# The u half of the spatial gate computed inside the attention, eight more merge gates in block products, and the two output projections run one after the other

## The reference

```python
h = rmsnorm(x, norm_mix_g)
q, kv, nsa_g, u, v, merge_g = split(h @ w_in)         # u, v: 1024 wide; merge_g: 2 x 2048
o_a = nsa_attention(q, compressed/selected/window k and v, sigmoid(nsa_g))      # 512 x 1024
v   = layernorm(gelu(v))                               # over 1024
o_b = gelu(u) * (tril(ws) @ v_chunk + bs)              # 8 groups of 128, chunks of 128 tokens
g   = sigmoid(merge_g)                                 # two branches
merged = g[0] * (o_a @ w_proj_a) + g[1] * (o_b @ w_proj_b)
x = x + merged @ w_mix_out
... cross attention over 256 memory tokens, SwiGLU, final norm
```

## Time and profile before

| | us |
|---|---|
| median of 3 runs | 2754.77 (2754.28 to 2754.85) |
| profiled execution | 2755.36 |
| its span | 2753.6 |
| TensorE busy in the span | 2712.6 (99%) |
| VectorE, ScalarE, GpSimd busy | 2105.9, 1209.4, 454.7 |

### The profile page before, as it was taken

How to read it: one execution, slowest core, us unless ns; L and a number is a source line. 1 busy time by engine, 2 the same in 40 slices (tenths; PEclk the granted TensorE clock), 3 DMA queues, 4 the chain that set the end, 5 groups by cost and what they waited for, 6 DMA issues and landing times.

```text
span 2753.6 us, 38090 instructions
## 1 busy us (share of the span) xinstructions
PE 2712.6 (99%) x14221; PEld 2301.0 (84%) x14221; DVE 2105.9 (76%) x2998; ACT 1209.4 (44%) x1923; POOL 454.7 (17%) x418
## 2 busy tenths in 40 slices
PE   8999999999999999999999999999999999999997
PEld 7888888888888888888877888888888888888886
DVE  6777874667755555555687899999999998988887
ACT  6444432766631222211154555555555555443334
POOL 0000002545520545411000000000000000010000
PEclk9999999999999999999999999999999999999999
DMA  7587867332233455444345788888889888999982
GB/s 240 139 187 177 205 157 171 81 89 62 54 96 104 102 145 150 133 115 114 92 142 138 172 216 198 218 208 212 196 214 215 207 207 250 300 305 297 302 262 93
DMA packets 647978, 479.38 MB, mean 174 GB/s; under 512 B 14484, under 2 KB 589320, under 8 KB 641928
## 3 DMA queue, kind: packets, MB, share of 16 engines
q1 hardware_dynamic: 568016, 416.58, 51.9%
q0 software_dynamic: 58896, 36.70, 10.2%
q10 hardware_dynamic: 20904, 23.92, 2.9%
HBM read 413.98 MB, written 63.18 MB: 173 GB/s over the span
## 4 chain that ended last, share of the span: by engine, by line
PE 85%; DVE 5%; ACT 3%; issue 2%; POOL 2%; DMA 2%; ACTq 0%; DVEq 0%; SPq 0%; POOLq 0%
PE banks L1405 10%; PE banks L1408 10%; PE banks L1406 9%; PE banks L976 9%; PE banks L978 9%; PE banks L977 9%; PE banks L1470 4%; PE banks L1472 4%; PE banks L1471 4%; PE banks L1074 3%; PE banks L1077 3%; PE banks L1075 3%; PE banks L1236 1%; PE banks L1237 1%; PE banks L1238 1%
## 5 line engine op out<-in xcount | busy, mean ns | idle before, releaser
L1487 DVE CAST w_hi<-raw 128x512 fp32r<-128x512 f32 (+1 forms) x232 | 141.5, 610 | 244.2 <-PE banks L978 171.4
L976 PE MATMUL banks<-act_hl,w_hi 128*128 128x512 f32 (+1 forms) x816 | 324.1, 397 | 2.5 <-DVE w_lo L1508 2.4
L977 PE MATMUL banks<-act_hl,w_hi 128*128 128x512 f32 (+1 forms) x816 | 319.0, 391 | 0.0
L978 PE MATMUL banks<-act_hl,w_lo 128*128 128x512 f32 (+1 forms) x816 | 318.9, 391 | 0.0
L1406 PEld LDWEIGHTS banks<-t_hl,wf_lo 128*128 128x128 f32 x1312 | 246.5, 188 | 58.1
L1405 PE MATMUL banks<-t_hl,wf_hi 128*128 128x512 f32 x656 | 259.5, 396 | 0.1
L1408 PE MATMUL banks<-t_hl,wf_hi 128*128 128x512 f32 x656 | 259.5, 396 | 0.0
L1406 PE MATMUL banks<-t_hl,wf_lo 128*128 128x256 f32 x1312 | 257.7, 278 | 0.0
L1940 DVE TENSOR_TENSOR wf_lo<-raw_f,wf_hi 128x1024 fp32r<-128x1024 f32 x164 | 200.3, 1221 | 55.8 <-ACT wf_hi L2586 55.7
L2586 ACT ACTIVATE wf_hi<-raw_f 128x1024 fp32r<-128x1024 f32 x164 | 173.8, 1060 | 137.6 <-PE banks L1408 82.0
L1406 PEld LDWEIGHTS banks<-tok_hl,wf_lo 128*128 128x128 f32 x984 | 184.9, 188 | 43.7
(11 more groups left out here) (357 smaller groups left out, 6574.1 us busy)
## 6 DMA issues: line engine op xcount, KB each, us to landing
raw_f<-in_w_ffn_in_dram SPq DMA_DIRECT2D x82, 1024.0 KB, 9.0
raw<-in_w_in_dram SPq DMA_DIRECT2D x42, 1024.0 KB, 5.6
h_full<-hidden_blocks SPq DMA_DIRECT2D x35, 1024.0 KB, 8.2
wo_raw<-in_w_ffn_out_dram SPq DMA_DIRECT2D x32, 1024.0 KB, 9.9
raw_g<-in_w_in_dram SPq DMA_DIRECT2D x26, 1024.0 KB, 8.7
hidden_blocks<-tok_hl SPq DMA_DIRECT2D x44, 512.0 KB, 6.3
s<-in_w_ffn_in_dram SPq DMA_DIRECT2D x40, 512.0 KB, 6.0
s<-in_w_ffn_in_dram POOLq DMA_DIRECT2D x40, 512.0 KB, 6.5
```

The source lines that it names most:

```text
L976: pe.matmul(dst, w_hi[:, q, j, 0:m], hi, start=first, stop=False)
L977: pe.matmul(dst, w_hi[:, q, j, 0:m], lo, start=False, stop=False)
L978: return pe.matmul(dst, w_lo[:, q, j, 0:m], hi, start=False, stop=last)
```

## The change

- The 8 panels of u move from `su` into the fill of the attention. Their raw result goes to DRAM (`su_dram`) and is loaded again by `rows_in`, as a fourth transfer of 256 KB behind the three small ones; GELU is then applied in place on SBUF.
- For them, 8 merge gates leave the fill and become 4 more pairs of block products (13 pairs become 17, 91 units become 119). The rotating buffers are renumbered.
- `su` is gone. `ab` is split in `pa` (all 16 half panels of branch a) and then `pb` (16 of branch b). The work of the 8 groups runs beside `pa`; PE mixes group n after half panel 2, 4, 5, 7, 9, 10, 12, 14.
- DVE multiplies each bank by its gate (`part_a`, `part_b`); POOL only adds and makes the low part. The gates come in 1 MB transfers of four tiles, and ACT applies the sigmoid tile by tile (`open_gate`): two tiles in each of the 8 rounds of the groups, four before the last group's copy, the rest beside `pb`.

```diff
-G_TILES = [...] + [("merge", n) for n in range(PLAIN_GATES, PLAIN_GATES + 10, 2)]
+G_TILES = [...] + [("merge", n) for n in range(PLAIN_GATES, PLAIN_GATES + 18, 2)]
+MIX_AT = {h: g for g, h in enumerate((2, 4, 5, 7, 9, 10, 12, 14))}
-        ("merge", (2 * DK - GATES_AHEAD,)), ("sv", (8,)), ("su", (8,)), ("ab", (16, 4, 2, 2)), ("wo", (16,)),
+        ("fill", (SG + 2 * DK - GATES_AHEAD,)), ("sv", (8,)), ("pa", (8, 4, 2, 2)), ("pb", (8, 4, 2, 2)), ("wo", (16,)),
...
 # SP
+            def gates_in(m):
+                b, c = divmod(m, 4)
+                if m >= 2:
+                    sp.wait_ge(gates_open, 4 * (m - 1))
+                if b:
+                    sp.wait_ge(banks_read, PH["pa"].group0 + 4 * c + 4)
+                rows = (b * DK + 4 * c) * P
+                sp.dma_start(gate_in[:, 4 * c:4 * c + 4], merge_dram[rows:rows + 4 * P].rearrange("(k p) t -> p k t", p=P)).then_inc(gates_landed[m % 2], 16)
...
 # PE
+            def half_panel(ph, h, hi, lo, ready, free=None):
+                pe.wait_ge(banks_read, ph.group0 + h - 1 if free is None else free)
...
+                for q in range(2):
+                    if h == 0:
+                        pe.wait_ge(ready, 4 * q + 4)
...
+            for h in range(16):
+                half_panel(PH["pa"], h, oa_hi, oa_lo, oa_lo_done, PH["sv"].group0 + TC if h == 0 else None)
+                if h in MIX_AT:
+                    mix(MIX_AT[h])
+            for h in range(16):
+                half_panel(PH["pb"], h, ob_hi, ob_lo, ob_lo_done)
...
 # DVE
+            def part_a(h):
+                dve.wait_ge(quarters_done, PH["pa"].quarter0 + 2 * h + 2)
+                dve.wait_ge(gates_open, h + 1)
+                dve.tensor_tensor(pa[:, h], bank[(PH["pa"].group0 + h) % 2][:], gate_in[:, h], ALU.mult).then_inc(banks_read, 1)
...
+            for h in range(16):
+                quarter_split(4 + 2 * h)
+                part_a(h)
+                quarter_split(5 + 2 * h)
+                if h == 14:
+                    dve.wait_ge(mix_copied, SG)
...
+            for h in range(16):
+                if h < 14:
+                    quarter_split(36 + 2 * h)
+                part_b(h)
+                if h < 14:
+                    quarter_split(37 + 2 * h)
...
 # ACT
+            def rows_in(n):
+                u = n % 2
+                for r, src in enumerate((sgu_ln_g[0], sgu_ln_b[0], sgu_b[0].rearrange("g t -> (g t)"))):
+                    act.dma_start(rows_bc[:, u, r], src[n * P:(n + 1) * P].partition_broadcast(P)).then_inc(rows_landed[u], 16)
+                act.dma_start(ut[:, u], su_dram[n * P:(n + 1) * P, :]).then_inc(rows_landed[u], 16)
...
+            for n in range(SG):
+                u = n % 2
+                wait(act, vn_done, n - 1)
...
+                act.wait_ge(rows_landed[u], n // 2 * 64 + 64)
+                act.activation(ut[:, u], ut[:, u], ACT.Gelu_apprx_tanh).then_inc(ut_done, 1)
+                open_gate(2 * n)
+                open_gate(2 * n + 1)
+                if n > 0:
+                    mix_out(n - 1)
+                if 0 < n < SG - 1:
+                    rows_in(n + 1)
+            for n in range(4):
+                open_gate(16 + n)
+            mix_out(SG - 1)
```

More of the change, by code:

```diff
@@ L779, in _ @@
             panel(PH["g"], 0, 0, [(0, 16, w_in_v[:, :, C_NSA_GATE:C_NSA_GATE + 48])])
-            columns(PH["merge"], w_in_v, C_MERGE + GATES_AHEAD * P)
+            for n in range(PH["fill"].n):
+                col = C_U + n * P if n < SG else C_MERGE + (GATES_AHEAD + n - SG) * P
+                panel(PH["fill"], *PH["fill"].at(n), [(0, 16, w_in_v[:, :, col:col + P])])
             ph = PH["sv"]
@@ L787, in _, with two_columns @@
                              w_in_v[:, 4 * k:4 * k + 4, C_V + b * T:C_V + (b + 1) * T]).then_inc(raw_landed[ph.slot(u)], 16)
[L788 to L804, removed]
+            def two_columns(ph, view, n):
+                panel(ph, *ph.at(n), [(8 * a, 8 * a + 8, view[:, :, (2 * n + a) * P:(2 * n + a + 1) * P]) for a in range(2)])
+            def gates_in(m):
[6 more added lines that the diff above has]
+                sp.dma_start(gate_in[:, 4 * c:4 * c + 4], merge_dram[rows:rows + 4 * P].rearrange("(k p) t -> p k t", p=P)).then_inc(gates_landed[m % 2], 16)
+            two_columns(PH["pa"], wa_v, 0)
+            two_columns(PH["pa"], wa_v, 1)
+            for b in range(2):
+                sp.wait_ge(gate_stored[b], 16 * (PH["m0"].n + PH["fill"].n) // 2)
+            sp.wait_ge(quarters_done, PH["sv"].end())
+            gates_in(0)
+            gates_in(1)
+            for n in range(2, 8):
+                two_columns(PH["pa"], wa_v, n)
+                if n in (3, 5):
+                    gates_in(2 + n // 5)
+            for n in range(8):
+                two_columns(PH["pb"], wb_v, n)
+                if n < 4:
+                    gates_in(4 + n)
             ph = PH["wo"]
@@ L1251, in _, with mix @@
                 token_rows(n)
-            ph = PH["su"]
-            def mix(n, u):
+            def mix(n):
+                u = n % 2
                 pe.wait_ge(vn_done, n + 1)
                 wait(pe, mix_copied, n - 1)
-                if isinstance(n, int) and n < 2:
+                if n < 2:
                     pe.wait_ge(banks_read, PH["sv"].groups_end())
                 for c in range(TC):
-                    mm = pe.matmul(bank[2 + u][:, c * P:(c + 1) * P], vn[:, u, c], ws_t[:, ds(n, 1), :],
+                    mm = pe.matmul(bank[2 + u][:, c * P:(c + 1) * P], vn[:, u, c], ws_t[:, n:n + 1, :],
@@ L1262, in mix @@
                                    start=True, stop=True)
                 mm.then_inc(mix_done, 1)
[L1264 to L1271, removed]
@@ L1274, in _ @@
[L1274 to L1284, removed]
@@ L1683, in _ @@
             query_low(0)
-            split(PH["merge"], 0, 0, quarters=range(AHEAD))
+            split(PH["fill"], 0, 0, quarters=range(AHEAD))
             dve.wait_ge(cmp_hi, 1)
@@ L2280, in gates_out @@
                 act.wait_ge(banks_read, ph.group0 + p + 1)
-                act.dma_start(merge_dram[tile * P:(tile + 1) * P, :], buf[:, n % 2]).then_inc(gate_stored[n % 2], 16)
+                act.dma_start(rows, buf[:, n % 2]).then_inc(gate_stored[n % 2], 16)
             def row_sums_high(k):
@@ L2447, in _ @@
                     p = k // 4
-                    if p < PH["merge"].n:
-                        high(PH["merge"], 0, p, k % 4)
+                    if p < PH["fill"].n:
+                        high(PH["fill"], 0, p, k % 4)
                     else:
@@ L2832, in _ @@
-            runs(pool, ph.n // 2, ab)
+                pool.tensor_tensor(ob_lo[:, n:n + 1, :], ob[:], ob_hi[:, n:n + 1, :].bitcast(F32), ALU.subtract).then_inc(ob_lo_done, 1)
+            for n in range(SG):
+                u = n % 2
+                pool.wait_ge(rows_landed[u], n // 2 * 64 + 64)
+                pool.wait_ge(vz_done, n + 1)
+                wait(pool, mix_done, n - 1)
+                pool.tensor_tensor(vz[:, u], vz[:, u], rows_bc[:, u, 0].unsqueeze(1).broadcast_to([P, TC, P]), ALU.mult).then_inc(vn_step, 1)
+                pool.wait_ge(vn_step, n + 1)
+                pool.tensor_tensor(vn[:, u], vz[:, u], rows_bc[:, u, 1].unsqueeze(1).broadcast_to([P, TC, P]), ALU.add).then_inc(vn_done, 1)
+                if n > 0:
+                    gate_out_tile(n - 1)
```

182 lines of the change are left out of this document (75 added, 107 removed).

## The result

The changed kernel takes 2763.69 us (median of 11 runs, 2761.91 to 2767.74), beside 2754.84 for the kernel before (11 runs, 2753.85 to 2758.43) in the same session: ratio 1.0031, 95% interval 1.0022 to 1.0040, or 8.9 us. The forecast was 2756.3, the range up to 2764.0. So the time lies in the range, but only by 0.3 us, and beyond what counts as no change: "slower by over 0.2%" had a chance of 0.27 against 0.59 for no change. It came out where the case "the landing grows" put it (2763.5), and beyond the far end of the forecast's own sum (2761.1 at T = 13.6). The profiled execution after has a span of 2762.0, before 2753.6: 8.4 us to be explained.

The account below looks back on a forecast made before the run. The prediction took TensorE, busy at eight or nine tenths in nearly every slice, to bound the kernel. The stretch up to `wo` at -76.5 us and four more pairs at +78.0 gave +1.5, a forecast of 2756.3, range 2749.3 to 2764.

Parts of the forecast that it names:

- the landing grows: Slower rival: rows and u tile land later beside 1 MB weight and gate loads; landing 7.3, 2763.5 us, chance 0.18.
- T: Length of one turn of a group's round on ScalarE, copy to next copy: 12.7 to 12.8 us, between 11.9 and 13.6.
- Four pairs at 19.51, +78.0: The four added block pairs run at the pace of the twelve behind the first, 19.51 us each, +78.0 in all.
- The work moved costs what it did before: The attention's fill stays at 16 panels and costs the same, with eight u panels in place of eight gates.
- Place 1: First gate, at half panel 2 of `pa`: TensorE waits 1.4 us for the bank VectorE multiplies, as ScalarE gets there late.
- Place 2: Round of a group beside `pa`: ScalarE's chain falls behind; TensorE waits 7.8 us in all, at mixes 5, 6 and 7.
- `ob_hi` to the landing, 6.1: Part of the round's turn: from making `ob_hi` until the next rows and u tile have landed, 5.2 plus 0.9 us.
- Place 3: End of `pb`: the first `wo` split is ready 2.0 us after the last matmul, costing TensorE 1.6 us.
- The sum: Stretch up to `wo` 192.6 us against 269.1, -76.5; with four pairs, +78.0, the total is +1.5 us.
- Faster: Rival: rounds hide under `pa` if the turn is 11.5 us or less; -6.3 us, 2748.5, chance 0.14.
- A switch drains ScalarE: Slower rival: a table switch drains ScalarE when a function follows at once; turn 14.2, 2764.6 us, chance 0.05.
- Block pairs don't repeat: Rival: each of the four added pairs takes the first pair's extra 1.3 us, +5.2 in all; 2761.5 us, chance 0.05.

Follow-up runs that it names:

- Thread only: The changed kernel with 13 block pairs instead of 17 and 24 panels (8 of u, 16 of gates) beside the attention: 2764.91 us, ratio 1.0036.
- the pair of kernels without waits: The changed kernel with u loaded early, four row buffers, gates opened before GELU and early `wo` splits: 2748.17 us with 17 block pairs, 2748.57 with 13.
- No u load: The changed kernel without the u tile's transfer for groups 2 to 7, which reuse the tiles of groups 0 and 1: 2754.21 us, ratio 0.9997.
- the best kernel: The changed kernel with u loaded early, four row buffers, gates opened before GELU and early `wo` splits, 17 block pairs: 2748.17 us, ratio 0.9977.
- gates first: The changed kernel with the two gates of each ScalarE round opened before GELU instead of behind it: 2764.41 us, ratio 1.0035.
- deep buffers: The changed kernel with u tiles loaded in two large transfers into their own places and four row buffers, rows asked three groups ahead: 2752.82 us, ratio 0.9993.

## Why the prediction was off, step by step

- **Four pairs at 19.51, +78.0.** Right: 332.93 - 254.90 = 78.0.
- **The work moved costs what it did before.** It does not, though this doesn't show in the forecast's total: the saving was booked as panels against pairs (87.1 - 78.0 = 9.1). Thread only shows that eight more panels beside the attention would have cost 79.7, so the pairs brought 1.7 at most, 0.5 in the pair of kernels without waits. I had not read the idle time of TensorE from k to `sv` in the kernel before, 4.9 us.
- **k and the attention unchanged.** Missed by 1.6, most of it a wait of 1.42 at 498.76 for VectorE's split in the first k panels; VectorE itself had waited for the panel's load. From the first pair to the first matmul of `pa` the six experiments with 17 pairs took 814.7 to 815.4 us where this execution took 816.0, so about half of the 1.6 belongs to this execution alone.
- **Place 1, 1.4.** Right: 1.35 of wait, 1.5 from start to start.
- **Place 2, 7.8.** The mechanism was right, and its size is what was off most. The term at fault is "`ob_hi` to the landing, 6.1". The trace of before held no transfer of the fourth kind; I bounded it by 5.2 and 6.9 and took a point between, reasoning that the tile "would be there before the rows if nothing queued". Measured: 6.8, with the fourth transfer the last to land. No u load shows that this transfer alone turns the result (2754.2 against 2763.7). The first copy came at 19.05 (18.8 forecast), the six turns took 80.55 (76.8), the tail behind the last turn 9.4 instead of 10.6, mostly because VectorE's first step on the last mix took 0.69 here, with POOL idle, and 1.52 before. So the chain ended 109.1 behind the start of `pa`, where the sum of these terms had 106.2. TensorE goes on at 109.10; in the best kernel, without place 1, it is there after 97.01. Of the 12.1 between, 1.5 are place 1 and 10.6 place 2, 2.8 more than forecast. TensorE spent them as 8.6 in waits (8.1 in the view of waits; 8.6 from the starts of its matmuls, 0.23 apart without a wait) and 1.6 at half clock, which was in no term but is not added on top, since the chain decides when it goes on. The waits stood at mixes 4 and 5, not at 5, 6 and 7; for the total this made no difference.
- **Place 3, 2.0 behind the last matmul.** 3.0 measured. VectorE's split here is no 0.69 as in the earlier trace rows:
```profile
1152.30 0.69 DVE L1793 TENSOR_TENSOR pb<-banks,gate_in 128x512 f32<-128x512 f32 x1 [4.76 <-PE banks L990]
...
1153.36 1.63 DVE L1493 TENSOR_TENSOR w_lo<-raw,w_hi 128x512 fp32r<-128x512 f32 x1
```
  POOL begins its own sum of `pb` and `pa` at 1153.07 and runs it for 1.37 us beside it. The prediction knew "up to 2 beside POOL" for the splits in `pb` and did not use it here. And 1.2 more at half clock behind it.
- **The sum.** Stretch: 181.4 + 1.5 + 10.6 + 3.0 = 196.5 of 196.6. With +78.0, +1.6 in k, attention and `sv` and +1.2 behind the start of `wo`, this gives +8.2 of 8.4. Against the forecast of +1.5, 2.8 come from place 2, 1.1 from places 1 and 3, 1.2 from half clock behind place 3, 1.7 from before the stretch. So place 2 as a whole is less than half of the miss: the turns added 3.8, nearly all by the landing, the later first copy 0.2, and the shorter tail took 1.2 back.
- **The rivals.** *The landing grows* had the number, but partly by luck. It named a landing of 6.8 as its threshold and priced one of 7.3. It was 6.8, for which the prediction's formula gives 2760.2 (T = 13.45); place 3, the clock behind it and the part before the stretch made up the difference. Nor was its reason, the gate loads of 1 MB, enough by itself: in no u load the landing went back to 5.3 with the gate loads in place. *Faster* was shown false by the turns. *A switch drains ScalarE*: not seen here either. The rows of this kernel are
```profile
966.20 1.28 ACT L2525 ACT_TABLE_LOAD   x1
967.49 0.63 ACT L2525 ACTIVATE ut<-ut 128x512 f32<-128x512 f32 x1
968.14 1.28 ACT L2516 ACT_TABLE_LOAD   x1
```
  with 0.01 and 0.02 us between end and start. By the Trainium skill, "ScalarE: Activation LUTs", section "What ACT_TABLE_LOAD costs", each switch would take 1.38 longer; the turn would then be 14.8, an estimate from the page's figure. The trace does not agree: 13.4 was measured. *Block pairs don't repeat*: false, 78.0.

## What to carry to other kernels

If an engine may only ask for data after it has used the last, and use waits for that data, the full time from issue to the last landing stands in every turn: count it with all transfers of the group queued one behind another, or break the loop with more buffers, which was worth 10.9 us here; taking single steps out of it was worth 9.5, 4.8 and nothing. Such a loop can have a twin on the next engine (here POOL, 1 us shorter), so an edit that takes more than that difference out of one gains little more than the difference: 0.2 and 0.5 us a turn here for 2.3 and 1.3 taken out. Work put beside a stage with idle time can cost less than its own pace, so price a stage's filling by its idle time before trading it for other work. And where a chain on other engines decides when TensorE goes on, time that it loses ahead of that point costs nothing more.

## What the hardware showed that I had not expected

TensorE's clock can fall behind a wait. Behind the wait of 6.96 us in the changed kernel, behind those of 3.32 and 4.29 in the kernel with gates first and those of 6.18 to 6.93 in three others, the first matmuls ran at 1.2 GHz, two to eight of them 0.42 us apart. The wait of 2.44 ahead of `wo` stands in six kernels, and six to eight slow matmuls followed in each; in deep buffers and in thread only four or five at full pace came first. There it costs 1.1 us on top of the wait, by the rest of the span in ten profiles. Waits of 1.09 to 1.74 us left the clock alone in six profiles. It isn't the length of the wait alone: one of 2.40 us, some 88 us from the start in all the kernels, was followed by full pace in six profiles, the one before the change among them, and by slow matmuls in four (deep buffers, thread only and the two best); what decides it is open. No wait of this kind stands in the stretch of the kernel before, so a new wait can cost more than its length, which that stretch could not have shown.
